# A two-layer decoder trunk on one core: weight splits, loads and memory value products put in another order at the boundaries

## The reference

```python
for l in range(DEPTH):                               # DEPTH = 2
    g = norm_g[l]
    h = rmsnorm(x, g[0])
    x = x + 0.5 * rmsnorm(swiglu(h, ffn_w_gate[l, 0], ffn_w_up[l, 0], ffn_w_down[l, 0]), g[1])
    h = rmsnorm(x, g[2])
    ...                                              # y = mixer(h): MLA + mLSTM in layer 0, sparse (DSA) in layer 1
    x = x + rmsnorm(y, g[3])
    h = rmsnorm(x, g[4])
    y = memory_cross_attention(h, rmsnorm(mem, mem_norm_g[l]), xa_wq[l], xa_wk[l], xa_wv[l], xa_wo[l])
    x = x + rmsnorm(y, g[5])
    h = rmsnorm(x, g[6])
    x = x + 0.5 * rmsnorm(swiglu(h, ffn_w_gate[l, 1], ffn_w_up[l, 1], ffn_w_down[l, 1]), g[7])
```

## Time and profile before

| | |
|---|---|
| median of 3 runs | 1220.72 us |
| the profiled execution, its device time | 1216.88 us |
| its span, first to last instruction | 1215.2 us |
| PE busy | 1128.0 us, 93% of the span |
| DVE busy | 669.8 us, 55% |
| ACT busy | 564.6 us, 46% |
| mean granted TensorE clock | 0.981 |

### The profile page before, as it was taken

One profiled execution on the slowest core, in us unless ns is written; L12 is line 12 of the kernel. 1 busy time (PEld: TensorE's weight loads), 2 busy tenths in 40 slices (PEclk: granted clock), 3 DMA queues, 4 the chain that ended last, 5 costly groups with the idle time before them and its releaser, 6 DMA issues.

```text
span 1215.2 us, 18613 instructions
## 1 busy us (share of the span) xinstructions
PE 1128.0 (93%) x7634; PEld 1034.7 (85%) x7634; DVE 669.8 (55%) x829; ACT 564.6 (46%) x794; POOL 73.2 (6%) x168
## 2 busy tenths in 40 slices
PE   4799999999879899999999999999988888999997
PEld 4799999896769798999989999998856877899997
DVE  3555554662786656554564554546565655554553
ACT  5444343634646655443353544335444654543341
POOL 2100000110011020000010000002100102000000
PEclk9899999999989999999999999999989998999999
DMA  7365555542425354656545656555153343466551
GB/s 229 124 202 195 190 166 166 158 139 87 139 94 166 121 175 146 224 185 205 172 141 163 225 185 201 168 164 163 45 159 104 114 147 121 143 207 205 175 172 69
DMA packets 144348, 193.08 MB, mean 159 GB/s; under 512 B 3270, under 2 KB 127116, under 8 KB 144284
## 3 DMA queue, kind: packets, MB, share of 16 engines
q1 hardware_dynamic: 143020, 187.93, 47.7%
q0 software_dynamic: 1264, 4.25, 1.1%
HBM read 191.12 MB, written 1.05 MB: 158 GB/s over the span
## 4 chain that ended last, share of the span: by engine, by line
PE 80%; DVE 9%; ACT 6%; DMA 2%; issue 2%; POOL 1%; SPq 0%; ACTq 0%; POOLq 0%; DVEq 0%
PE psum L767 20%; PE psum L671 15%; PE psum L673 15%; PE psum L672 15%; PE psum L922 4%; DVE w_lo L1736 2%; PE psum L754 2%; ACT w_hi L1187 2%; PE psum L682 2%; PE psum L684 2%; PE psum L683 2%; DVE x_state L1778 1%; PE psum L817 1%; ACT w_hi L1183 1%; PE psum L913 1%
## 5 line engine op out<-in xcount | busy, mean ns | idle before, releaser
L1736 DVE TENSOR_TENSOR w_lo<-raw,w_hi 128x2048 fp32r<-128x2048 f32 x162 | 370.9, 2289 | 155.2 <-ACT w_hi L1187 154.8
L671 PE MATMUL psum<-h_hi,w_hi 128*128 128x256 f32 x1568 | 446.3, 285 | 6.7 <-DVE h_lo L1756 6.7
L673 PE MATMUL psum<-h_hi,w_lo 128*128 128x256 f32 x1568 | 444.7, 284 | 0.0
L672 PE MATMUL psum<-h_lo,w_hi 128*128 128x256 f32 x1568 | 444.7, 284 | 0.0
L1187 ACT ACTIVATE w_hi<-raw 128x2048 fp32r<-128x2048 f32 x162 | 310.0, 1916 | 233.1 <-DMA raw<-in_ffn_w_gate 129.9
L671 PEld LDWEIGHTS psum<-h_hi,w_hi 128*128 128x128 f32 x1568 | 301.9, 193 | 9.4 <-issue 7.6
L672 PEld LDWEIGHTS psum<-h_lo,w_hi 128*128 128x128 f32 x1568 | 301.8, 192 | 1.9 <-issue 0.2
L673 PEld LDWEIGHTS psum<-h_hi,w_lo 128*128 128x128 f32 x1568 | 301.8, 192 | 0.0
L767 PE MATMUL psum<-w_hi,g_both 128*128 128x512 f32 x640 | 184.9, 401 | 12.7 <-DVE w_lo L1736 12.7
L767 PEld LDWEIGHTS psum<-w_hi,g_both 128*128 128x128 f32 x640 | 119.4, 191 | 39.2 <-issue 13.4
L1825 DVE TENSOR_TENSOR work<-psum,lat 128x512 f32<-128x512 f32 x44 | 30.4, 691 | 156.3 <-PE psum L673 137.1
(11 more groups left out here) (255 smaller groups left out, 1230.3 us busy)
## 6 DMA issues: line engine op xcount, KB each, us to landing
raw<-in_ffn_w_gate SPq DMA_DIRECT2D x44, 1024.0 KB, 5.3
raw<-in_ffn_w_up SPq DMA_DIRECT2D x44, 1024.0 KB, 5.3
raw<-in_ffn_w_down SPq DMA_DIRECT2D x44, 1024.0 KB, 4.9
raw<-in_ab_w_in SPq DMA_DIRECT2D x9, 1024.0 KB, 5.4
gain_row<-in_norm_g POOLq DMA_DIRECT2D x8, 512.0 KB, 6.1
raw<-in_xa_wk SPq DMA_DIRECT2D x4, 1024.0 KB, 5.4
raw<-in_ab_w_out SPq DMA_DIRECT2D x4, 1024.0 KB, 4.9
raw<-in_xa_wq SPq DMA_DIRECT2D x4, 1024.0 KB, 5.4
```

What stands on the lines that cost most here:

```text
L671: nc.tensor.matmul(o, wh, a_hi[:, k, :], start=(k == 0), stop=False)
L672: nc.tensor.matmul(o, wh, a_lo[:, k, :], start=False, stop=False)
L673: last = nc.tensor.matmul(o, wl, a_hi[:, k, :], start=False, stop=(k == KT - 1))
L1736: nc.vector.tensor_tensor(w_lo[:, c % RING, 0:k * n], raw[:, c % RAWS, 0:k * n], w_hi[:, c % RING, 0:k * n].bitcast(F32), ALU.subtract).th ...
```

## The change

1. **Start.** SP issues `norm_g` first, then x, G0.0, U0.0, `mem`, and the nine parameter arrays last. POOL's load of the first gain row goes behind the norm factors of x. PE transposes `norm_g` alone before x; the parameters are transposed behind the row factors. ACT and DVE split both halves of x before the first weight. The memory is transposed between U0.0 and G0.1, and split before D0.0.
2. **First down weights.** In all four feed-forward layers D0 is split before the row factors and the passage of the first pair. A one-element silu ahead of it makes ACT load its table there.
3. **Boundaries.** PE transposes x[0] before both chunks of y[1]'s second half, six matmuls of 512 columns earlier than now. At the end of a cross attention the squares and the gain of y[0] go before the split of the last two attention outputs. At a mixer's boundary all of x[0]'s split goes before the last square.
4. **Memory values of layer 1.** `xv1.0` becomes the fill before sub-layer 5, `xv1.1` the fill before 6. In the second cross attention nothing is left between the scores. Before 6, the first half of the fill stands between y[0] and y[1], and none between y[1] and the transposes of x[1].
5. Some buffers move in SBUF.

```diff
-FILL = {1: "xk0.0", 2: "xk0.1", 3: "xk1.0", 4: "xk1.1", 6: "xv1.0"}
-XA_FILL = [["xv0.0", "xv0.1"], ["xv1.1"]]
+FILL = {1: "xk0.0", 2: "xk0.1", 3: "xk1.0", 4: "xk1.1", 5: "xv1.0", 6: "xv1.1"}
+XA_FILL = [["xv0.0", "xv0.1"], []]
...
         def _(sp):
+            sp.dma_start(grow[:, :], A['norm_g'].rearrange("l j (k p) -> (l j k) p", p=P)).then_inc(gain_load, 16)
             for t in range(NT):
                 sp.dma_start(x[:, t, :], A['x'][0, P * t:P * (t + 1), :]).then_inc(x_load[t], 16)
...
                     load(c)
-                    if c == 0:
-                        load_parameters()
                     if c == 1:
                         sp.dma_start(stage, A['mem'][0].rearrange("(t p) n -> p t n", p=P)).then_inc(mem_load, 16)
+                        load_parameters()
...
-                        if half and final and s + 1 in RAW_INPUT:
+                        if half and n == 0 and s + 1 in RAW_INPUT:
                             input_transposes(s + 1, 0)
...
             last_downs_0(last_rows("co", 4)[1:])
+            out_ = fill(6, 0)
             ready(f"pv{us[-1]}")
             last_downs_1(last_rows("co", 4), 5)
-            cross(1, 6)
+            cross(1, 6, out_)
...
                     if fill:
                         split_to(last + 2)
-                    square_half(1, 0)
+                    square_half(s, last, 1, 0)
                     input_hi(s + 1, 0, [0])
-                    square_half(1, 1)
-                    input_hi(s + 1, 0, [1])
                     if s + 1 in MIXERS:
+                        input_hi(s + 1, 0, [1])
+                        square_half(s, last, 1, 1)
                         split_to(last + 2)
+                    else:
+                        square_half(s, last, 1, 1)
+                        input_hi(s + 1, 0, [1])
                     square(f"pre{s + 1}", 0, x[:, 0, :])
                     input_hi(s + 1, 1)
                     split_to(last + 2 + fill)
...
                     if p:
                         hi_half(c + 1, i)
                     act_hi(p, i)
-                    if (s, p) == (0, 0):
-                        mem_hi()
-                    hi_half(c + 2, i)
+                    if p:
+                        hi_half(c + 2, i)
 
                 split_to(c0 + 3)
+                if s == 0:
+                    mem_hi()
+                nc.scalar.activation(small[:, 23, 0:1], gcol[:, 0:1], ACT.Silu)
+                split_to(c0 + 4)
                 act.wait_ge(rbc_full, FFNS[s] + 1)
                 nc.scalar.activation(rbc, psum[:, 0, 0:TOK], ACT.Copy).then_inc(rbc_done, 1)
...
                 prob_copy(u2)
                 prob_copy(u3)
+                last = C[f"xo{l}.1"]
+                square_half(s, last, 0, 0)
+                square_half(s, last, 0, 1)
                 output_hi(u2)
                 output_hi(u3)
...
             input_hi(0, 0)
+            input_hi(0, 1)
             split_to(0)
-            input_hi(0, 1)
             split_to(1)
...
+            split_to(C["co.3"] + 1)
             output_hi(us[-1])
             boundary(5, C["co.3"])
```

More of the change, by code:

```diff
@@ L169, in cross @@
         xv = XA_FILL[l]
-        out.extend([f"xq{l}.0", f"xq{l}.1", f"score{u[0]}", f"score{u[1]}", xv[0], f"score{u[2]}", f"pT{u[0]}"] +
+        out.extend([f"xq{l}.0", f"xq{l}.1", f"score{u[0]}", f"score{u[1]}"] + xv[:1] + [f"score{u[2]}", f"pT{u[0]}"] +
                    xv[1:] + [f"pT{u[1]}", f"score{u[3]}", f"pv{u[0]}", f"pv{u[1]}",
@@ L298, in build @@
         pT = work[:, 2048:3072].rearrange("p (a h k n) -> p a h k n", a=2, h=2, k=2)
-        grow, prow = work[:, 0:P], work[0:64, P:2 * P]
+        grow, prow = work[:, 2048:2048 + P], work[0:64, 2304:2304 + P]
         rin = work[:, 0:640].rearrange("p (t h n) -> p t h n", t=NT, h=5)
@@ L719, in fill, with begin @@
                 return out_
-            def begin(s):
-                out_ = fill(s, 0)
+            def begin(s, out_=None):
+                if out_ is None:
+                    out_ = fill(s, 0)
                 if s == 0:
@@ L858, in ffn @@
                 feature_major(f"U{s}.0", h_hi, h_lo)
+                if s == 0:
+                    memory_transposes()
                 for p in range(PEEL):
@@ L923, in up, with cross @@
                 filled(name, last)
-            def cross(l, s):
+            def cross(l, s, out_=None):
                 u0, u1, u2, u3 = units_of(f"xa{l}")
-                begin(s)
+                begin(s, out_)
                 feature_major(f"xq{l}.0", h_hi, h_lo, gate=s)
@@ L934, in cross @@
                 xv = XA_FILL[l]
-                token_major(xv[0], m_hi, m_lo)
+                for name in xv[:1]:
+                    token_major(name, m_hi, m_lo)
                 scores(u2)
@@ L1220, in input_hi, with square_half @@
                         ins.then_inc(h_hi_done, 1)
+            def square_half(s, last, t, half):
+                if t == 0:
+                    act.wait_ge(y0_full, s + 1)
+                elif half == 0:
+                    act.wait_ge(y1_half, s + 1)
+                else:
+                    act.wait_ge(down_done, n_down[last])
+                square(f"post{s}", t, y[:, t, 512 * half:512 * (half + 1)], half)
             def boundary(s, last):
@@ L1358, in cross @@
                 exps(u1)
-                split_to(C[XA_FILL[l][-1]])
+                split_to(C[([f"xq{l}.1"] + XA_FILL[l])[-1]])
                 split_to(C[f"xo{l}.0"])
                 xv = XA_FILL[l]
-                evacuate_memory(xv[0])
+                for name in xv[:1]:
+                    evacuate_memory(name)
                 prob_copy(u0)
@@ L1374, in cross @@
                 prob_copy(u3)
+                last = C[f"xo{l}.1"]
+                square_half(s, last, 0, 0)
+                square_half(s, last, 0, 1)
                 output_hi(u2)
                 output_hi(u3)
-                boundary(s, C[f"xo{l}.1"])
-            act.wait_ge(*full("gains"))
-            nc.scalar.activation(gcol[:, :], bank("gains")[:, 0:P], ACT.Copy)
-            evacuate("gains", pcol[:, 0:NP], bank("gains")[:, P:P + NP])
+                boundary(s, last)
+            evacuate("gains", gcol[:, :], bank("gains")[:, 0:P])
             act.wait_ge(*freed["gains"])
             input_hi(0, 0)
+            input_hi(0, 1)
             split_to(0)
-            input_hi(0, 1)
             split_to(1)
@@ L1857, in ffn @@
                 split_to(c0 + 3)
+                if s == 0:
+                    mem_lo()
+                split_to(c0 + 4)
                 dve.wait_ge(rbc_done, FFNS[s] + 1)
```

61 lines of the change are left out of this document (32 added, 29 removed).

## The result

| | before | after |
|---|---|---|
| median of 4 runs each, us | 1220.49 (1219.85 to 1220.81) | 1211.41 (1210.69 to 1211.88) |
| ratio, 95% interval | | 0.9926 (0.9909 to 0.9943) |
| profiled execution, its span, us | 1216.88, 1215.2 | 1211.88, 1210.2 |
| mean granted clock | 0.981 | 0.974 |

The change makes the kernel 9.1 us faster; 2.1 were forecast. Between the two profiled executions it is only 5.0 us, at a lower clock.

The account below looks back on a forecast made before the run. TensorE was taken as the bound, so gains come from its idle time or clock. Terms -13.4 - 8.4 + 2.8 + 1.0 + 8.8 + 7.1 = -2.1 us take the median 1220.72 to 1218.6, range 1211.5 to 1224.5.

Parts of the forecast that it names:

- start with D0.0: Start of layer 0: G0.0 begins at 14.8, D0.0 at 43.4 without 2.0 us of low clock; -13.4 us, bounds -8.5 and -15.
- other first down weights: Layers 3, 4, 7: 6.3 us of waits for D0 go, and the low clock behind them; -8.4 us, bounds -6.3 and -8.5.
- buffers in SBUF: Buffers that move in SBUF change no instruction, so they were given no term in the sum.
- rival 3: At the start, norm_g needs 8.9 us in any place, so ACT starts 3.9 us later: 1222.5 us; chance 10%.
- x[0] six matmuls earlier: Boundaries into 2 and 4: PE comes 1.4 us earlier and waits 1.4 more for x[0]; +2.8 us, bounds 0 and +2.8.
- Into the sparse mixer: Boundary into 5: PE waits 2.1 us for x[0] and idles 6.1 before `c.1`; shift +10.8, 5.8 of it moved work.
- Rival 1: At the boundary into the sparse mixer `c.1` is no stall, so 6.1 and 2.0 go: 1210.5 us; chance 13%.
- Out of it: Out of the sparse mixer: PE waits 2.7 us for `xv1.1`, 3.2 for x[1], none for x[0]; shift +1.1 (-1 to +3).
- Inside the cross attention: Second cross attention: without the 5.8 us fill the down product comes at 988.0 instead of 991.15; -3.1 us (0 to -5.8).
- The clock: Low clock behind six new stalls: 2.0 at `c.1`, 1.7 before x[1] out of the mixer, 3.4 for four shorter; +7.1 us.
- Rival 4: Low clock behind all six new stalls, short ones in full, long ones at 3.4 each: slower, 1225.1 us; chance 15%.
- Rival 2: The short stalls keep the clock, as the 2.28 us wait in layer 3 did: -3.4, 1215.2 us; chance 12%.

Follow-up runs that it names:

- parts 1 and 2 alone: The kernel before with the new start and the first down weights split early in all four feed-forward layers, nothing else: 1196.54 us, ratio 0.9806.
- The experiment: The kernel after with the sparse mixer's second chunk, `c.1`, split ahead of x[1] on ACT and DVE: 1204.16 us, ratio 0.9870 to the kernel before.
- the four built on parts 1, 2 and 5: The kernel before with these parts: unaltered 1191.97 us; `vaug`, `ident` and following buffers aligned to 64 bytes 1191.96; `w` 64 bytes askew 1171.32; `h` askew 1181.94.

## Why the prediction was wrong

The sum was -2.1 and the result -9.1. Part by part:

| term | forecast | measured |
|---|---|---|
| start with D0.0 | -13.4 | -13.5 (24.4 less 10.9) |
| other first down weights | -8.4 | -10.9 |
| buffers in SBUF | 0 | -4.6 to -6.6 |
| parts 3 and 4, with their clock | +19.7 | +19.4 (1191.97 to 1211.41; 20.0 by the ratios) |

**The step that failed** stands in the part on the start: "the buffers that move in SBUF change no instruction". That is true, but no reason to put the term at nothing: a down product of the same 24 instructions takes 5.47 instead of 5.62 us when `g_both` stands elsewhere, and that one edit is worth 5.5 to 6.6 us. I costed it at zero without bounds, and the range had no room for it. With the 5.5 us of its ratio the forecast would have been 1213.1, and 1211.41 inside a range moved along with it. No experiment leaves the rest of the miss to one term: parts 3 and 4 together came within 1 us of their sum.

**A term of the right sign that was probably too small** is the other first down weights. The 6.3 us of waits went. The clock's share was read from one execution, 0.2 in layer 3 where another paid 1.8 (7.38 less 5.62), and my bound of -8.5 came from the same single profile. The medians say 10.9, but the interval of the ratio, 8.3 to 11.6, still holds 8.4. Adding 3.8 us for "under the median of the runs" was a patch over the same thing: the longer executions differ by their clock, and in layer 3 the change takes away a wait that can cost it.

**Start.** The steps came as forecast: G0.0 at 14.90 (14.8), D0.0 at 44.09 (43.4), with a wait of 1.2 (0.4 to 2); its product still took 5.73, and 7.42 in the kernel with parts 1 and 2 alone, so the 2.0 us of low clock are not surely gone. PE's wait for `norm_g` ended at 2.78, rival 3 falls. The prediction read `norm_g` as what held the start back; before, the wait was ended by another of the small arrays, which PE doesn't wait for there any more:

```profile
PE psum L964 <- DMA work<-in_mem_norm_g: 12.3, 1, 12.3
```

The silu table took 1.28 again and the small silu ended 0.2 behind it.

**x[0] six matmuls earlier.** Waits of 1.30, 2.33 and 2.34 for 1.4, 2.1 and 2.1: right. Undoing it gives 2.6 to 3.2. At the cross attentions the waits for the last attention output ahead of y[1] (L755, L754 before) are 2.7 us where they were 1.9: 0.8 for 1.0.

**Into the sparse mixer.** 6.04 for 6.1, ending at 832.56: 847.2 less the 14.8 by which the last down products of layer 4 start earlier (802.47 for 817.26) is 832.4. The experiment gave 7.3 us (6.8 by the ratios), so about 1 us of clock besides the stall (2.0 forecast). Rival 1 falls.

**Out of it.** Waits of 2.68 (2.7) and 3.23 (3.2), none for x[0]: right.

**Inside the cross attention.** From the start of the scores to the down product it is 12.22 us now and was 15.66, a gain of 3.4 for a forecast of 3.1.

**The clock.** 6.6 us in four stretches for 7.1 in six stalls looks right, but that is partly luck. The boundary out of the mixer had paid before, behind its wait of 2.67 us, so one of the two 1.7 there is not new. And the boundary 0 to 1, which the forecast didn't price, now pays 1.7 behind a wait of 1.95 us. The stretches before:

```profile
230.34:238.34 8.00, 7.65 (x63) 7.44 (x64) 6.15 (x14) 4.57 (x11) 1.04 (x2) 1.00 0.92 288
952.83:960.83 8.00, 7.63 (x44) 6.95 (x45) 6.57 (x11) 3.90 (x12) 1.71 (x4) 0.79 0.66 219
```

and the one at 0 to 1 after:

```profile
216.64:224.64 8.00, 8.00 (x53) 7.73 (x54) 5.55 (x12) 3.47 (x11) 1.04 (x2) 0.79 0.90 287
```

This goes with the buffers and not with the order of the lists. The wait for x's low part there is 1.93 to 2.02 us in the ten profiles whose down product takes 5.47 to 5.49 us, and 1.61 to 1.71 in the other ten. None of the latter paid. Six of the former did, the kernel before with the buffers moved among them; the four built on parts 1, 2 and 5 did not. That the stalls of 2.33 and 2.34 us differ, and the same 2.28-us wait of before paid 0.2 once and 1.8 once, says that a price per stall holds only on average. Rival 4 (every new stall paid, the long ones at 3.4) falls: two of six paid nothing, none over 1.7. Rival 2 (the four short stalls keep the clock) is half right: the one into 4 is the only short one that pays anew, since the fill into 6 stands where 1.7 were paid already.

## What to carry to other kernels

A buffer that only moves is a change: compare the time of the same product on both chains before anything else (the mean of a group on the page mixes in the clock), and try a few offsets of the large operands of TensorE, since no rule found here says which is good. One profile is one draw of the clock; where timed runs spread more than the profile's distance to the median, profile again before pricing a stall. An order that is written by chunk number (`last + 2`) silently means another chunk once a fill is put in front. And parts of a change are worth timing apart: parts 1, 2 and 5 alone take 1191.97 us, and parts 3 and 4 give 19.4 of that back.

## What was not expected of the hardware

- The place of an operand in SBUF moves matmul spacing by 2 to 5%: a down product 5.47 us with `g_both` 0 or 256 bytes beyond a multiple of 512, and 5.58 to 5.62 at 16, 32, 64, 80 and 128; 96 gate and up products 11.51 us with `w` and `h` at multiples of 512, 11.31 with `h` 64 bytes on, 10.91 with `w` 64 bytes on, and in layer 3 of that kernel 11.31.
- The granted clock after equal stalls in equal surroundings differs: 0.80 and 1.00 in the stretches behind 2.33 and 2.34 us; behind the wait of some 6 us at the start, the first 8.1 us of products ran at 0.70 to 0.79 in eight of the fifteen profiles with part 1 and at 1.00 in seven; in executions of the kernel before, 1.00 and 0.83 behind the first down wait of layer 3.
